# Prompt attention: probabilities turned against a diagonal of reciprocals, values as weights

## The chip, the cores and the metric

One core of one Trainium2 chip runs the whole program. The metric is the device time of one execution in microseconds (us), the median of several. The core's engines are TensorE (PE in the rows, its weight loads PEld), VectorE (DVE), ScalarE (ACT), GpSimd (POOL) and SyncE (SP), which issues most DMAs; each runs its own instruction list in order and waits on semaphores.

## The reference

Two hybrid decoder layers for a prompt of 528 rows (16 learned + 512) and 64 sample rows. In each layer the prompt's attention is two head groups over the same queries:

```
# sparse group (DSA), 8 heads x 64, one shared K/V head
score = sum over 8 index heads of w * relu(q_idx . k_idx), causal; keep the top_k = 528 // 4 = 132 best
s = q . k * 64**-0.5, keys not chosen -> -inf
o_a = softmax(s) @ v                      # v: 64 wide
# latent group (MLA), 8 heads, latent 128
s = (q_lat . c_kv + q_pe . k_pe) * scale, causal
o_lat = softmax(s) @ c_kv                 # 128 wide
o_b = o_lat @ w_uv                        # 128 -> 64 per head
mix = concat(o_a, o_b) @ w_o
```

## The kernel before, in words

A layer runs as blocks with a barrier of all engines between them: the index block, `prompt_block`, two sample blocks, the dense block. The change is in `prompt_block` alone, which is passed twice (once a layer). Between two blocks GpSimd clears a range of semaphores.

`prompt_block` cuts the 528 query rows into tiles t = 0..3 of 128 rows and t = 4 of 16 rows; tile t sees (t+1) x 128 keys. A *group* is a kind and a tile ("M" latent, "D" sparse), in the order M0, D0, M1, D1, ... M4, D4. A *unit* is one head of one group, so 8 units a group (one for t = 4, where the 8 heads lie stacked in the rows): 66 units a layer. A table `plan` sets the order by hand. In iteration i every engine does its part of several units:

- PE: sometimes an index product for a later tile (L1720), the scores of unit i (L1739 to L1745), the *turn* of unit i-1 (L1754: the exponentials `pP` transposed with the identity, one matmul per 128 keys), the *sum* of unit i-2 (L1772: weights are the turned probabilities `pPT`, values move through; out comes rows x values). At a group's end it also turns the group's scaled outputs (`posb`, L1791) and, for M, multiplies with `wuv` (L1783).
- DVE: row maximum of unit i (L1916); *rounds* that find the best keys of a later D group (L1883, L1885, eight a round, 0 to 2 rounds a unit by a table); at a group's end reciprocals of the 8 row sums (L1928) and the scaling of all 8 heads' outputs (L1937, L1933); a step of the sample group's selection in 14 units (L1478, L1481); the low parts `xtl` (L1865).
- ACT: relu of the index product (L1826), exponential with row sum of unit i (L1833), copy of the turned unit i-1 (L1843), copies `polT` (L1854) and `xth` (L1808) at group ends.
- POOL: weights and adds the index scores in 24 units of t = 0 and 1 (L1665, L1668, L1671), then, once PE has reached the last M3 unit, issues the gather of the first cache page for the next block (L1674, recorded as L1980).

Score products use two PSUM slots in turn, turned blocks two others, and the sums lie in banks 6 and 7. The exponentials have three buffers, `pPT` two.

The lines that order the turn and the sum:

```
1751  e.wait_ge(S.s_read, plan[u]["s"] + 1)      # turn of u waits for its exponential
1754  mm = e.transpose(BB(q)[0:kr, ...], Pb[:, u % 3, k * P:k * P + kr], T.ident[:, :])
1761  e.wait_ge(S.o_done, o_free[kind, t])       # first sum of a group waits for the scaling
```

Of the kernel before, what the change touches and what calls it, by code (L numbers as in the profile page):

```python
# [5 lines left out]
F32 = mybir.dt.float32  # L6
# [8 lines left out]
P = 128  # L15
# [924 lines left out]
def proj_stage(nc, T, S, l, W, O, B, S0_, ln_e):  # L940
# [50 lines left out]
    if True:  # L991
# [307 lines left out]
        def tensor(e):  # L1299
# [142 lines left out]
            for name, b, who in TURNS[JOB["ql2"]:]:  # L1442
# [45 lines left out]
def prompt_block(nc, T, S, next_cache):  # L1488
# [36 lines left out]
    osb = T.M.put("posb", [P, 1024], F32, A.region(4096))  # L1525
# [10 lines left out]
    rinv = T.M.put("prinv", [P, 2, 9], F32, A.region(72))  # L1536
# [24 lines left out]
    lag = n + 6  # L1561
    for i in range(lag):
        p = dict(idx=None, dots4=None, sum4=None, s=None, t=[], pv=None, norm=None, ot=[], uv=None)
# [19 lines left out]
        if i - 2 in last:  # L1583
            p["norm"] = last[i - 2]
        if i - 4 in last and last[i - 4][0] == "M":
            p["uv"] = (b_job, last[i - 4][1])
            b_kind.append("X")
            b_job += 1
        if i - 3 in last:
            kind, t = last[i - 3]  # L1590
            for a in range(2 if kind == "M" and t < 4 else 1):
                p["ot"].append((b_job, kind, t, a))
                b_kind.append("O" if kind == "M" else "X")
                b_job += 1
        plan.append(p)
    tjob = {i - 1: p["t"][-1] for i, p in enumerate(plan) if p["t"]}
    ot_job = {(kind, t): q for p in plan for q, kind, t, a in p["ot"]}
# [30 lines left out]
    with nc.Block() as block:  # L1628
# [10 lines left out]
        def _(e):  # L1639
# [11 lines left out]
            for i, p in enumerate(plan):  # L1651
# [3 lines left out]
                if p["idx"]:  # L1655
# [10 lines left out]
                    else:  # L1666
# [4 lines left out]
                        e.tensor_tensor(sc, sc, re, ALU.add).then_inc(S.scored, 1)  # L1671

# [4 lines left out]
        def _(e):  # L1677
# [15 lines left out]
            for i, p in enumerate(plan):  # L1693
# [53 lines left out]
                for part, q in enumerate(p["t"]):  # L1747
                    u = i - 1
                    kind, t, h = units[u]
                    if part == 0:  # L1750
                        e.wait_ge(S.s_read, plan[u]["s"] + 1)
                    b_free(e, q)
                    for k, kr in key_tiles(t)[4:] if part else key_tiles(t)[:4]:
                        mm = e.transpose(BB(q)[0:kr, (k % 4) * P:(k % 4 + 1) * P], Pb[:, u % 3, k * P:k * P + kr], T.ident[:, :])  # L1754
                    mm.then_inc(S.b_ps, 1)
                if p["pv"] is not None:
# [10 lines left out]
                    for k, kr in kts:  # L1767
                        if k < 4:
                            v = T.z[0:kr, k, at_v:at_v + w]
                        else:  # L1770
                            v = vt[0:16, 0:AD] if kind == "D" else vt[0:16, AD:AD + RL]
                        mm = e.matmul(flat[:, o:o + w], PT[0:kr, u % 2, k * P:(k + 1) * P], v,  # L1772
                                      start=k == kts[0][0], stop=k == kts[-1][0])
                    mm.then_inc(S.pv_done, 1)
                if p["uv"]:
# [3 lines left out]
                    e.wait_ge(S.b_out, sum(1 for x in b_kind[:ot_job["M", t] + 1] if x != "X"))  # L1779
# [6 lines left out]
                for q, kind, t, a in p["ot"]:  # L1786
                    e.wait_ge(S.o_done, at[kind, t] + 1)
                    b_free(e, q)
                    for k in range(4 if t < 4 else 1):
                        c = (4 * a + k) * P  # L1790
                        mm = e.transpose(BB(q)[:, k * P:(k + 1) * P], osb[:, c:c + P], T.ident[:, :])  # L1791
                    mm.then_inc(S.b_ps, 1)

        def mix(q, kind, t):

            cols = slice(QC[t], QC[t] + QT[t])
            if (kind, t) == ("D", 4):
                return [((half_rows(u), slice(0, 4), cols), BB(q)[half_rows(u), 64 * u:64 * u + 64].rearrange("p (k c) -> p k c", k=4))
                        for u in range(2)]
            return [((slice(0, P), slice(4, 8) if kind == "M" else slice(0, 4), cols),  # L1800
                     BB(q).rearrange("p (k c) -> p k c", k=4)[:, :, 0:QT[t]])]

        @block.scalar
        def _(e):
            def mix_hi(q, kind, t):
                e.wait_ge(S.b_ps, q + 1)
                for to, src in mix(q, kind, t):
                    ins = e.activation(T.xth[to], src, ACT.Copy)  # L1808
                ins.then_inc(S.mix_hi, 1)

            for i, p in enumerate(plan):
# [23 lines left out]
                for part, q in enumerate(p["t"]):  # L1835
# [8 lines left out]
                    else:  # L1844
                        e.activation(PT[0:16, u % 2, 512:PW], BB(q)[0:16, 0:P], ACT.Copy).then_inc(S.b_out, 1)
                if p["uv"]:
                    mix_hi(p["uv"][0], "M", p["uv"][1])
                for q, kind, t, a in p["ot"]:
                    if kind == "D":
                        mix_hi(q, kind, t)  # L1850
                    else:
                        e.wait_ge(S.b_ps, q + 1)
                        nh = 4 if t < 4 else 1
                        e.activation(olT[:, 4 * a:4 * a + nh, :], BB(q)[:, 0:nh * P].rearrange("p (k c) -> p k c", k=nh), ACT.Copy)\  # L1854
                         .then_inc(S.b_out, 1)
# [1013 lines left out]
```

## Time and profile before

| | us |
|---|---|
| median of 3 runs (lowest, highest) | 3161.12 (3158.76, 3161.49) |
| the profiled execution | 3156.46 |
| its span | 3154.7 |
| first prompt block in it | 644.4 to 832.2, 187.8 |
| second prompt block begins, next block's first work | about 2195, 2385.2 |

Over the whole span PE is busy 93%, DVE 45%, ACT 32%, POOL 20%; the granted clock of PE is 9 tenths or more nearly everywhere. The prompt blocks are a different program from the rest: there PE and DVE work in turns on short instructions, so a share over the span tells little about them. They are read from windows and timelines of the first block; the second repeats it row by row (the row maximum at 819.70 of the first stands at 2372.70 in the second).

### The profile page before, as it was taken

What the parts mean: (1) busy time and instruction counts of PE and PEld (TensorE: products, weight loads), DVE (VectorE), ACT (ScalarE), POOL (GpSimd) and SP (SyncE); (2) the same over time, 40 slices, a digit from 0 to 9 for tenths busy, and PEclk for the clock granted to TensorE, in tenths of its full rate; (3) what the DMA queues carried; (4) which work ended last, traced back from release to release, by engine and by line L of the source; (5) the groups of instructions that cost most, each with busy time, mean ns of one, the idle gap of its engine ahead of it and who ended that gap; (6) DMA issues with size and microseconds to landing.
All of it is one profiled execution on the core that took longest, in us unless ns stands there. A gap on an engine that the chain in (4) does not pass through costs nothing. (4 is left out here: it accounts for less than half of the span.)

```text
span 3154.7 us, 45592 instructions
## 1 busy us (share of the span) xinstructions
PE 2939.6 (93%) x18282; PEld 2524.9 (80%) x18298; DVE 1413.7 (45%) x2118; ACT 998.4 (32%) x1620; POOL 643.3 (20%) x562
## 2 busy tenths in 40 slices
PE   7999999888898899999999999998888988999997
PEld 7999879755566689998799997795656666999975
DVE  2222255579764442223632223735887445222236
ACT  2222233454443332222422222334444333122223
POOL 1111021330113141110221110412302123211103
PEclk9999999999999999999999999999999999999998
DMA  4222452400123322224422224423002234222243
GB/s 118 80 80 80 134 158 79 144 1 1 68 86 131 107 87 80 80 80 135 160 87 80 80 86 141 144 62 134 1 18 80 74 113 147 73 80 79 88 147 124
DMA packets 241737, 293.79 MB, mean 93 GB/s; under 512 B 12624, under 2 KB 205488, under 8 KB 235456
## 3 DMA queue, kind: packets, MB, share of 16 engines
q1 hardware_dynamic: 234688, 229.00, 23.6%
q0 software_dynamic: 6912, 62.92, 5.4%
q8 instruction: 91, 1.49, 0.2%
q14 instruction: 46, 0.38, 0.0%
HBM read 287.72 MB, written 3.88 MB: 92 GB/s over the span
## 5 line engine op out<-in xcount | busy, mean ns | idle before, releaser
L159 DVE TENSOR_TENSOR wlo<-raw,whi 128x1024 fp32r<-128x1024 f32 (+2 forms) x398 | 515.0, 1295 | 1298.1 <-ACT whi L153 1296.9
L153 ACT ACTIVATE whi<-raw 128x1024 fp32r<-128x1024 f32 (+2 forms) x398 | 418.6, 1053 | 1438.7 <-PE ps L608 864.8
L608 PE MATMUL ps<-xth,whi 128*128 128x296 f32 x2624 | 752.2, 299 | 5.4 <-PEq L770 5.4
L608 PE MATMUL ps<-xtl,whi 128*128 128x296 f32 x2624 | 754.7, 300 | 0.0
L608 PE MATMUL ps<-xth,wlo 128*128 128x296 f32 x2624 | 571.7, 300 | 0.0
L608 PEld LDWEIGHTS ps<-xth,whi 128*128 128x128 f32 x2624 | 494.7, 189 | 5.5 <-issue 5.5
L608 PEld LDWEIGHTS ps<-xtl,whi 128*128 128x128 f32 x2624 | 493.5, 188 | 0.0
L608 PEld LDWEIGHTS ps<-xth,wlo 128*128 128x128 f32 x2624 | 427.5, 188 | 0.0
L166 PE MATMUL ps<-whi,hth 128*128 128x512 f32 (+1 forms) x880 | 350.6, 398 | 10.0 <-DVE wlo L159 8.4
L168 PE MATMUL ps<-whi,htl 128*128 128x512 f32 (+1 forms) x880 | 346.9, 394 | 0.0
L167 PE MATMUL ps<-wlo,hth 128*128 128x512 f32 (+1 forms) x880 | 346.7, 394 | 0.0
L575 POOL CAST hth<-hf 128x592 f32 x88 | 59.8, 680 | 930.3 <-DVE hf L534 889.6
L166 PEld LDWEIGHTS ps<-whi,hth 128*128 128x128 f32 (+1 forms) x880 | 158.5, 180 | 67.8 <-DVE wlo L159 22.2
L168 PEld LDWEIGHTS ps<-whi,htl 128*128 128x128 f32 (+1 forms) x880 | 158.2, 180 | 45.9
L167 PEld LDWEIGHTS ps<-wlo,hth 128*128 128x128 f32 (+1 forms) x880 | 158.4, 180 | 42.1
L166 PE MATMUL ps<-whi,xth 128*128 128x338 f32 (+3 forms) x370 | 135.7, 367 | 15.1 <-DVE wlo L159 13.1
L262 POOL TENSOR_SCALAR x<-x,rstd,nb 128x1024 f32<-128x1024 f32 (+2 forms) x24 | 30.7, 1278 | 560.6 <-DVE nb L253 560.6
L577 POOL TENSOR_TENSOR htl<-hf,hth 128x592 f32 x88 | 129.4, 1470 | 14.5 <-POOL hth L575 14.5
L167 PE MATMUL ps<-wlo,xth 128*128 128x338 f32 (+3 forms) x370 | 130.9, 354 | 0.0
L168 PE MATMUL ps<-whi,xtl 128*128 128x338 f32 (+3 forms) x370 | 130.8, 354 | 0.0
L1833 ACT ACTIVATE pP<-ps,pnmx 128x128 f32<-128x128 f32 (+3 forms) x132 | 70.3, 533 | 182.1 <-DVE pnmx L1916 182.1
L1772 PE MATMUL ps<-z,pPT 128*128 128x128 f32 (+1 forms) x672 | 97.6, 277 | 10.8 <-DVE posb L1937 10.8
(407 smaller groups left out, 4348.0 us busy)
## 6 DMA issues: line engine op xcount, KB each, us to landing
raw<-in_ffn_w_in SPq DMA_DIRECT2D x176, 512.0 KB, 3.8
raw<-in_ffn_w_out SPq DMA_DIRECT2D x176, 512.0 KB, 3.5
raw<-in_w_o SPq DMA_DIRECT2D x32, 512.0 KB, 3.4
raw<-in_w_in SPq DMA_DIRECT2D x16, 507.0 KB, 3.9
gb<-in_ln_g SPq DMA_DIRECT2D x6, 512.0 KB, 5.6
gb<-in_ln_b SPq DMA_DIRECT2D x6, 512.0 KB, 6.4
raw<-in_w_in SPq DMA_DIRECT2D x8, 338.0 KB, 3.1
x<-in_x_prompt SPq DMA_DIRECT2D x1, 1536.0 KB, 10.7
```

Of the source, the lines that this page charges most:

```text
L153: e.activation(dst, T.raw[:, s, 0:width], ACT.Copy).then_inc(S.hi_done, 1)
L159: e.tensor_tensor(w_lo, T.raw[:, s, 0:width], w_hi.bitcast(F32), ALU.subtract).then_inc(S.split_done, 1)
L166: e.matmul(out, lhi, rhi, start=start, stop=False)
L167: e.matmul(out, lhi, rlo, start=False, stop=False)
L168: return e.matmul(out, llo, rhi, start=False, stop=stop)
L262: e.tensor_scalar(x, x, T.rstd[0:r, t:t + 1], T.nb[0:r, t:t + 1], ALU.mult, ALU.add).then_inc(S.norm_done, 1)
L575: e.tensor_copy(h_hi, T.hf[:, u, :]).then_inc(S.hhi_done, 1)
L577: e.tensor_tensor(h_lo, T.hf[:, u, :], h_hi.bitcast(F32), ALU.subtract).then_inc(S.hlo_done, 1)
L608: mm = e.matmul(bank(u, up)[:, h, :], part[:, s, w], xp[:, k, o], start=(k == 0 and part is T.whi and xp is T.xth), stop=(k == KD - 1 and ...
L1772: mm = e.matmul(flat[:, o:o + w], PT[0:kr, u % 2, k * P:(k + 1) * P], v, start=k == kts[0][0], stop=k == kts[-1][0])
L1833: e.activation(Pb[:, i % 3, 0:NK[t]], SB(p["s"], P, NK[t]), ACT.Exp, bias=nmx[:, i % 3:i % 3 + 1], accum_out=rsum[:, a, c:c + 1]).then_inc ...
```

## The change

Per unit: DVE takes the reciprocal of the unit's row sum right behind the unit's exponential; POOL multiplies the identity with it into a 128x128 diagonal `pdiag` (three buffers); PE's turn becomes a full float32 product of `pP` (weights) with that diagonal, so the probabilities come out turned and already scaled. The sum then takes the values as weights and the turned probabilities as the moving side, so outputs come out turned. At group ends the scaling on DVE, `posb` and its turns on PE are gone; ACT copies from the sums' banks straight to `polT` (M) or `xth` (D). The product with `wuv` comes one iteration earlier. The prompt block's semaphores are now aliased on the dense block's set, not the sample block's.

```diff
@@ PE
                     if part == 0:
-                        e.wait_ge(S.s_read, plan[u]["s"] + 1)
+                        e.wait_ge(S.diag_done, u + 1)
                     b_free(e, q)
                     for k, kr in key_tiles(t)[4:] if part else key_tiles(t)[:4]:
-                        mm = e.transpose(BB(q)[0:kr, (k % 4) * P:(k % 4 + 1) * P], Pb[:, u % 3, k * P:k * P + kr], T.ident[:, :])
+                        mm = e.matmul(BB(q)[0:kr, (k % 4) * P:(k % 4 + 1) * P], Pb[:, u % 3, k * P:k * P + kr], diag[:, u % 3, :],
+                                      start=True, stop=True)
...
-                    if h == 0 and o_free[kind, t] > 0:
-                        e.wait_ge(S.o_done, o_free[kind, t])
+                    if h == 0:
+                        sums_free(e, kind, t)
...
-                        mm = e.matmul(flat[:, o:o + w], PT[0:kr, u % 2, k * P:(k + 1) * P], v,
-                                      start=k == kts[0][0], stop=k == kts[-1][0])
+                        for out, c in sums(kind, t, h):
+                            mm = e.matmul(out, v, PT[0:kr, u % 2, k * P + c.start:k * P + c.stop],
+                                          start=k == kts[0][0], stop=k == kts[-1][0])
...
-                for q, kind, t, a in p["ot"]:
-                    e.wait_ge(S.o_done, at[kind, t] + 1)
-                    b_free(e, q)
-                    for k in range(4 if t < 4 else 1):
-                        c = (4 * a + k) * P
-                        mm = e.transpose(BB(q)[:, k * P:(k + 1) * P], osb[:, c:c + P], T.ident[:, :])
@@ new: where a sum goes (D: even heads to rows 0-63, odd to 64-127), and what its bank waits for
+    def sums(kind, t, h):
+        if t == 4:
+            if kind == "M":
+                return [(flat[:, 7 * 512:7 * 512 + P], slice(0, P))]
+            return [(flat[half_rows(u), 6 * 512:6 * 512 + 64], half_rows(u)) for u in range(2)]
+        if kind == "M":
+            return [(flat[:, 6 * 512 + h * P:6 * 512 + (h + 1) * P], slice(0, P))]
+        c = 6 * 512 + h // 2 * P
+        return [(flat[half_rows(h % 2), c:c + P], slice(0, P))]
+    def sums_free(e, kind, t):
+        if (kind, t) == ("M", 4):
+            e.wait_ge(S.ol_out, 8)
+        elif kind == "D" and t < 4:
+            e.wait_ge(S.ol_out, 2 * t + 1)
+        elif t > 0:
+            e.wait_ge(S.d_lo, t)
+            if kind == "M":
+                e.wait_ge(S.ol_out, 2 * t)
@@ POOL, at the end of every iteration and ahead of the page gather
+                if i < n:
+                    e.wait_ge(S.rinv_done, i + 1)
+                    e.tensor_scalar(diag[:, i % 3, :], T.ident[:, :], rinv[:, i % 3:i % 3 + 1], 1.0, ALU.mult, ALU.mult)\
+                     .then_inc(S.diag_done, 1)
@@ ACT: sums_out at a group's end
+                e.wait_ge(S.pv_done, i - 1)
+                if kind == "D":
+                    e.activation(T.xth[to], src, ACT.Copy).then_inc(S.d_hi, 1)
...
+                    for a in range(2):
+                        e.activation(olT[:, 4 * a:4 * a + 4, :], T.ps[:, 6 + a, :].rearrange(...), ACT.Copy).then_inc(S.ol_out, 1)
@@ DVE
+                    of, k = rounds.get(units[i], (0, 0))
+                    now = min(k, 1)
                     if units[i] in rounds:
-                        now = 1 if p["norm"] else k
                         choose(of, now, i == starts[of], i == ends[of] and now == k)
-                if p["norm"]:
...
+                    e.wait_ge(S.s_read, p["s"] + 1)
+                    if i >= 3:
+                        e.wait_ge(S.diag_done, i - 2)
+                    e.reciprocal(rinv[:, i % 3:i % 3 + 1], rsum[:, a, c:c + 1]).then_inc(S.rinv_done, 1)
+                if p["out"] and p["out"][0] == "D":
+                    mix_lo(None, *p["out"], S.d_hi, S.d_lo)
                 if i < n:
-                    if p["norm"] and units[i] in rounds and now < k:
+                    if now < k:
                         choose(of, k - now, False, i == ends[of])
@@ build
-        prompt_s, index_s, init_s = (Again(sample_s, names) for names in (PROMPT_SEMS, INDEX_SEMS, INIT_SEMS))
+        index_s, init_s = (Again(sample_s, names) for names in (INDEX_SEMS, INIT_SEMS))
+        prompt_s = Again(dense_s, PROMPT_SEMS)
```

PE's order from the last M3 unit into D3, before (`pP` exponentials, `pPT` turned ones, `posb` scaled outputs, `z` values):

```order
L1744 MATMUL ps<-kT_89,qaT 128x512
L1745 MATMUL ps<-pbias,identb 128x512
L1754 MATMUL ps<-ident,pP 128x128 x4
L1772 MATMUL ps<-z,pPT 128x64 x4
L1791 MATMUL ps<-ident,posb 128x128 x8
```

The same place in the changed kernel:

```order
L1757 MATMUL ps<-pkeys_3858,qaT 128x512
L1758 MATMUL ps<-pbias,identb 128x512
L1767 MATMUL ps<-pdiag,pP 128x128 x4
L1786 MATMUL ps<-pPT,z 128x128 x4
L1757 MATMUL ps<-kT_89,qaT 128x512
L1758 MATMUL ps<-pbias,identb 128x512
L1767 MATMUL ps<-pdiag,pP 128x128 x4
L1786 MATMUL ps<-pPT,z 64x128 x4
L1797 MATMUL ps<-polT,wuv 64x128 x8
L1757 MATMUL ps<-pkeys_3858,qaT 128x512
```

The turn reads `pdiag`, the sum has its operands exchanged, the eight turns of `posb` are gone and the product with `wuv` stands one iteration earlier.

DVE in units M3 h0 and h1, before:

```order
L1916 TENSOR_REDUCE pnmx<-ps 128x1
L1878 TENSOR_TENSOR pwork_3845<-pwork_3845,trib 16x16
L1883 MAX ptop<-pwork_3845 16x8
L1885 MATCH_REPLACE pwork_3845<-ptop,pwork_3845 16x532
L1883 MAX ptop<-pwork_3845 16x8
L1885 MATCH_REPLACE pwork_3845<-ptop,pwork_3845 16x532
L1916 TENSOR_REDUCE pnmx<-ps 128x1
L1883 MAX ptop<-pwork_3845 16x8
L1885 MATCH_REPLACE pwork_3845<-ptop,pwork_3845 16x532
L1928 RECIPROCAL prinv<-prsum 128x8
L1937 TENSOR_TENSOR posb<-ps,prinv 128x512
```

And changed:

```order
L1924 TENSOR_REDUCE pnmx<-ps 128x1
L1886 TENSOR_TENSOR pwork_3845<-pwork_3845,trib 16x16
L1891 MAX ptop<-pwork_3845 16x8
L1893 MATCH_REPLACE pwork_3845<-ptop,pwork_3845 16x532
L1934 RECIPROCAL prinv<-prsum 128x1
L1891 MAX ptop<-pwork_3845 16x8
L1893 MATCH_REPLACE pwork_3845<-ptop,pwork_3845 16x532
L1924 TENSOR_REDUCE pnmx<-ps 128x1
L1891 MAX ptop<-pwork_3845 16x8
L1893 MATCH_REPLACE pwork_3845<-ptop,pwork_3845 16x532
L1934 RECIPROCAL prinv<-prsum 128x1
L1874 TENSOR_TENSOR xtl<-ps,xth 128x4x128
```

Every unit has a reciprocal behind its first round; the scaling is gone, and D2's low part follows in h1.

POOL at the end of the block, before:

```order
L1671 TENSOR_TENSOR pwork<-pwork,prelu 128x512
L1654 MEMSET pwork_3845 128x4
L1980 DMA pg<-in_cache_mla,rows 128x2560
L1628 UNCONDITIONAL_BRANCH
L1951 ISA
```

And changed:

```order
L1683 TENSOR_SCALAR pdiag<-ident,prinv 128x128 x13
L1663 MEMSET pwork_3845 128x4
L1683 TENSOR_SCALAR pdiag<-ident,prinv 128x128 x22
L1974 DMA pg<-in_cache_mla,rows 128x2560
L1637 UNCONDITIONAL_BRANCH
```

The gather of the next block's page stands behind the last diagonal.

## Rows read from the trace of the kernel before

**Rows 1.** Windows: us, PE, PEld, DVE, ACT, POOL busy (count), PEclk, DMA, GB/s.

```profile
644.40:678.17 33.77, 28.15 (x166) 20.78 (x167) 23.10 (x58) 17.56 (x65) 17.01 (x32) 0.90 0.01 1
678.17:717.90 39.73, 36.04 (x209) 25.41 (x208) 34.24 (x92) 21.27 (x63) 20.26 (x23) 1.00 0.01 1
717.90:745.26 27.36, 21.21 (x115) 13.95 (x114) 26.15 (x60) 8.81 (x26) 0.10 (x1) 1.00 0.00 1
745.26:766.53 21.27, 19.76 (x132) 14.01 (x133) 18.08 (x38) 11.36 (x29) 0.00 (x0) 1.00 0.01 2
766.53:794.56 28.03, 26.34 (x139) 16.65 (x139) 27.14 (x52) 10.52 (x26) 1.05 (x1) 1.00 0.10 33
794.56:820.45 25.89, 22.32 (x147) 15.53 (x148) 21.94 (x39) 11.82 (x28) 0.00 (x0) 1.00 0.04 17
820.45:832.20 11.75, 8.83 (x76) 6.78 (x75) 3.78 (x11) 4.97 (x14) 0.00 (x0) 0.97 0.01 1
644.40:832.20 187.80, 162.65 (x976) 113.09 (x979) 154.43 (x345) 86.31 (x247) 38.42 (x56) 0.98 0.02 8
```

**Rows 2.** Timeline inside group D2: start us, us, engine, line, instruction.

```profile
761.23 0.56 DVE L1916 TENSOR_REDUCE pnmx<-ps 128x1 f32<-128x384 f32 x1
...
761.66 0.86 PE L1744 MATMUL ps<-pkeys,qaT 128*128 128x384 f32 x2
...
761.82 0.58 ACT L1833 ACTIVATE pP<-ps,pnmx 128x384 f32<-128x384 f32 x1 [0.94 <-DVE pnmx L1916]
...
762.30 0.19 ACT L1833 ACTIVATION_READ_ACCUMULATOR pP<-ps,pnmx 128x1 f32 x1
...
762.51 0.68 DVE L1885 MATCH_REPLACE8 pwork<-ptop,pwork 128x516 f32<-128x516 f32 x1
...
762.55 0.55 PE L1754 MATMUL ps<-ident,pP 128*128 128x128 f32 x3
...
762.93 0.88 PE L1772 MATMUL ps<-z,pPT 128*128 128x64 f32 x6
763.22 0.56 DVE L1916 TENSOR_REDUCE pnmx<-ps 128x1 f32<-128x384 f32 x1
```

**Rows 3.** Timeline inside group M3, TensorE.

```profile
784.65 1.02 PE L1739 MATMUL ps<-ckvT,qlatT 128*128 128x512 f32 x2
...
786.42 0.60 PE L1754 MATMUL ps<-ident,pP 128*128 128x128 f32 x4
...
786.87 1.06 PE L1772 MATMUL ps<-z,pPT 128*128 128x128 f32 x8
...
787.76 1.02 PE L1739 MATMUL ps<-ckvT,qlatT 128*128 128x512 f32 x2
```

**Rows 4.** Waits in the block: who waited for whom, us in total, times, longest.

```profile
PE ps L1772 <- DVE posb L1937: 5.4, 6, 1.2
```

**Rows 5.** Groups by line in the block, VectorE: busy us, mean ns, idle before.

```profile
L1937 DVE TENSOR_TENSOR posb<-ps,prinv 128x1024 f32<-128x1024 f32 (+2 forms) x9 | 8.0, 884 | 0.8 <-PE ps L1791 0.5
...
L1928 DVE RECIPROCAL prinv<-prsum 128x8 f32<-128x8 f32 (+1 forms) x10 | 1.9, 195 | 2.9 <-PE ps L1772 2.6
```

**Rows 6.** Groups by line and shape in the block, GpSimd's scoring.

```profile
L1671 POOL TENSOR_TENSOR pwork<-pwork,prelu 128x512 f32<-128x512 f32 x7 | 8.9, 1272 | 0.6
...
L1668 POOL TENSOR_SCALAR prelu<-prelu,iw 128x512 f32<-128x512 f32 x7 | 4.9, 695 | 7.0 <-ACT prelu L1826 7.0
L1668 POOL TENSOR_SCALAR prelu<-prelu,iw 128x384 f32<-128x384 f32 x7 | 4.1, 588 | 4.5 <-ACT prelu L1826 4.5
```

**Rows 7.** GpSimd timeline: the page gather; then the landing of all gathers.

```profile
789.98 1.05 POOL L1980 DMA_INDIRECT pg<-in_cache_mla,rows  x1 [62.37 <-PE ps L1742]
...
DMA to landing us min/median/max: 6.2/6.6/10.3
```

**Rows 8.** The range clear at the end of the prompt block and of the dense block.

```profile
L1951 POOLq EVENT_SEMAPHORE_RANGE_CLEAR  x2: 196/196/196, 831.9 to 2384.9; - x2
...
L2814 POOLq EVENT_SEMAPHORE_RANGE_CLEAR  x3: 588/590/594, 595.8 to 3145.6; - x3
```

More of the change, by code:

```diff
@@ L1524, in prompt_block @@
     relu = T.M.put("prelu", [P, 2, PROMPT], F32, A.region(2 * PROMPT * 4))
-    osb = T.M.put("posb", [P, 1024], F32, A.region(4096))
+    rinv = T.M.put("prinv", [P, 3], F32, A.region(12))
+    diag = T.M.put("pdiag", [P, 3, P], F32, A.region(3 * P * 4))
     olT = T.M.put("polT", [P, 8, P], F32, A.region(4096))
@@ L1583, in prompt_block @@
         if i - 2 in last:
-            p["norm"] = last[i - 2]
-        if i - 4 in last and last[i - 4][0] == "M":
-            p["uv"] = (b_job, last[i - 4][1])
+            p["out"] = last[i - 2]
+        if i - 3 in last and last[i - 3][0] == "M":
+            p["uv"] = (b_job, last[i - 3][1])
             b_kind.append("X")
             b_job += 1
[L1589 to L1594, printed above, removed]
         plan.append(p)
     tjob = {i - 1: p["t"][-1] for i, p in enumerate(plan) if p["t"]}
-    ot_job = {(kind, t): q for p in plan for q, kind, t, a in p["ot"]}
     def b_free(e, q):
@@ L1778, in _ @@
                     b_free(e, q)
-                    e.wait_ge(S.b_out, sum(1 for x in b_kind[:ot_job["M", t] + 1] if x != "X"))
+                    e.wait_ge(S.ol_out, 2 * t + 2 if t < 4 else 9)
                     for h in range(8):
@@ L1845, in _, with mix_lo @@
                         e.activation(PT[0:16, u % 2, 512:PW], BB(q)[0:16, 0:P], ACT.Copy).then_inc(S.b_out, 1)
+                if p["out"]:
+                    sums_out(i, *p["out"])
                 if p["uv"]:
[L1847 to L1855, printed above, removed]
+                    latent_hi(*p["uv"])
         @block.vector
         def _(e):
-            nround, nlo, nsround = [0], [0], [0]
-            def mix_lo(q, kind, t):
-                nlo[0] += 1
-                e.wait_ge(S.mix_hi, nlo[0])
-                for to, src in mix(q, kind, t):
-                    ins = e.tensor_tensor(T.xtl[to], src, T.xth[to].bitcast(F32), ALU.subtract)
-                ins.then_inc(S.mix_lo, 1)
+            nround, nsround = [0], [0]
+            def mix_lo(q, kind, t, high, low):
+                e.wait_ge(high, t + 1)
+                to, src = mix(q, kind, t)
+                e.tensor_tensor(T.xtl[to], src, T.xth[to].bitcast(F32), ALU.subtract).then_inc(low, 1)
             def choose(t, k, start, end):
```

63 lines of the change are left out of this document (20 added, 43 removed).

## The prediction

> **What bounds the kernel now.** The windows by group come first, since both prompt blocks are separate from the rest by barriers: what they gain or lose goes into the time one to one, twice. The reader sees 187.8 us for the first block, PE busy 162.7 and DVE 154.4, ACT 86, POOL 38 [rows 1]. Neither of the two is full, so the wait that ends last changes by group: in M2 DVE is busy 26.15 of 27.36 us and PE 21.2; in D2 both are near (18.1 and 19.8 of 21.3); in M3 27.1 and 26.3 of 28.0.
>
> Second, a timeline inside D2, which shows the beat of one unit. The row maximum starts at 761.23, the next one at 763.22: 1.99 us. In it DVE does maximum and one round back to back, until 763.19, so DVE sets the beat. PE meanwhile does scores from 761.66, turn at 762.55, sum at 762.93. The turn starts 0.06 after the exponential's row sum ended (762.49), and could come no earlier [rows 2]. In M3 PE goes without a pause: scores 784.65, turn 786.42, sum 786.87, next scores 787.76, 3.11 us a unit [rows 3]. There four turns take 0.45, and eight passes of the sum 0.89: 0.111 us a pass of 128 columns.
>
> Third, the waits: `posb` held PE's sums 6 times, 5.4 us in all [rows 4]. That is the stall which the change removes, with the DVE work behind it.
>
> **What is removed, per block.** DVE: the scalings, 8.0 us, and 10 reciprocals, 1.9 us [rows 5]. PE: 50 turns of `posb` at 0.111, 5.5 us, and the 5.4 us of waits. What is late next there: for D groups, an ACT copy and `xtl` in place of reciprocal and scaling, both of which were there before; for M, the ACT copy alone. I give these ends the full DVE gain and no more.
>
> **What is added, per block.**
> 1. *Turns as products.* A turn was one pass per 128 keys (4 in the M3 unit), the float32 sum of the same size is two (8) [rows 3]. The product with the diagonal has the sum's shape, so it takes two: 0.111 more per key block, 160 blocks in t = 0 to 3 and 8 or so in t = 4, 18.6 us of PE. Net of `posb`'s turns PE gets 13 us more work. Sums keep their passes (for D, weights of 128 columns and 64 moving become weights of 64 and 128 moving; six passes of a D2 sum are recorded with 0.88 us [rows 2], eight of an M3 sum with 128 moving with 1.06 [rows 3], so the narrow side saved nothing and its exchange costs nothing).
> 2. *Reciprocals.* 66 on DVE. One costs 0.16 to 0.2 (10 took 1.9, [rows 5]); with its gap I take 0.2: 13.2 us. Net of what is removed: +3.3 us. In a unit without a round DVE now also stands until the exponential is done: in D2 the row sum ends 1.26 us after the maximum began, and the maximum itself takes 0.56 [rows 2]: 0.7 us of standing. Seven units carry a selection step and no round (five in t = 0, two in D3), and what is queued behind is the step and then the next maximum, which ACT and, through ACT, PE wait for.
> 3. *Diagonals.* 66 on POOL. No such instruction is in the trace. By the scoring multiply, 0.695 us for 512 keys and 0.588 for 384 [rows 6], 0.107 per 128, a 128-wide one takes 0.37; its ends are 0.17 (a quarter of the 512-wide one) and 0.59 (the 384-wide one, if width did not matter below it). I take 0.37, since both rows lie on that slope. In 24 units POOL is also scoring: 0.695 + 1.272 ahead of the diagonal at 512 keys.
> 4. *The longer way to the turn.* This decides. Before: from a unit's maximum to its turn 1.32 us (761.23 to 762.55, [rows 2]). Now: maximum and round until 763.19 (1.96), reciprocal 0.2, diagonal 0.37, two hand-overs of 0.06: 2.65 us. PE then does turn, sum and the scores of the unit after the next, and only these give DVE its next maximum. So two beats cannot be shorter than 2.65 + turn 0.67 + sum 0.67 + scores 0.89 + 0.1 = 4.98, one beat 2.49, where it was 1.99.
>
> **Group by group**, per block, by the longest of DVE's work, PE's work and the loop of point 4:
> - D2 (21.27): DVE 1.99 + 0.2 = 2.2 a unit, PE 0.89 + 0.33 + 0.67 + 0.33 = 2.2, loop 2.49. Six units at +0.5, less the scaling at M2's end: a scaling and its reciprocal take 0.88 + 0.2 = 1.1 on average [rows 5], after an M group, twice as wide, I take 1.4, after a D group 0.8; about half of it is on the path here, since the loop now ends last: **+2.2**.
> - M3 (28.03): PE 3.11 + 0.44 = 3.55 a unit, 28.4 for eight, and it still stands about 1 us while DVE has its units of two rounds; DVE has 27.1 - 0.8 + 1.6 = 27.9. So 29.3: **+1.3**.
> - D3 (25.89): the loop is 2.8 + 0.89 + 0.89 + 1.1 + 0.1 over two, 2.9, against 2.1 of DVE (D2's 1.99 and 0.1 for the wider maximum) in three units without a step, +2.4; standing 0.7 in two, +1.4; less the scaling 1.4, the 8 turns of `posb` 0.9, and 1.1 of posb's waits: **+0.4**.
> - M2 (27.36): DVE bound; 8 x 0.2 less 0.85: **+0.8**.
> - t = 1 (39.73): 16 reciprocals 3.2, less 2.3 for the scalings; PE +3.5 of passes less 1.3; in D1 POOL needs 1.97 + 0.37 + gaps, 2.5 us a unit, where the mean was 2.6 with units at 2.0. **+2.7**, between -1 and +7.
> - t = 0 (33.77): five step units at 0.7, reciprocals 3.2, passes 1.8, less 1.5; the product of these hides half: **+3.2**, between 0 and +5.
> - t = 4 (11.75): the way M4, D4 to the end loses two scalings and two turns with their hand-overs, and gains longer turns (1.1) and diagonals: **-0.8**.
> - The clear of semaphores between blocks: 0.196 us for the prompt block's set, 0.590 for the dense one, which it now shares [rows 8]: **+0.4**.
> - The page gather moves from 789.98 to behind the last diagonal, some 6 us before the block's end; it lands 6.2 to 10.3 us after its issue, median 6.6 [rows 7]. What waits for it is the next block's first instructions on PE and ACT. At the median it is just late, **+0.1**; at 10.3 +3.8.
>
> Sum 10.3 us a block, 20.6 for two. The ends, taken together, are -4 and +28 a block: t = 0 and 1 as given (-1, +12), the other terms between what DVE alone gives them (-3 in all) and every unit at its loop with a diagonal of 0.59 and the late page (+16). The profiled execution took 3156.5, so 3177.1; the median of the runs stands 4.6 above it, and I forecast for that: **3181 us**, +0.65%.
>
> The trace's price of a turn, one pass against two, is what I use, and its block gives 18.6 us of added PE work. The Trainium skill (page "TensorE: Matmul & The Clock Gate", Terms) says of the transpose mode that it is 4x faster for FP32; by that rule the lost mode would cost three more passes each, 56 us a block, which is a rival below. Another page, "TensorEngine Tiling (Array Packing)", When to Use Tiling, names just this exchange: with a 64-wide right side, swap the operands and get two column tiles. By it D's sums, 80 key blocks of two passes, would cost half, 8.9 us of PE less a block. No row shows it here, and heads whose halves differ stand a whole iteration apart in PE's order, so I count nothing for it.
>
> **The rivals.**
> - *A. PE's passes hide and the group ends pay: faster.* PE is idle 25 of 187.8 us, DVE 33 [rows 1]. If the diagonal is always there when PE comes to the turn (it stands behind the next unit's scores, 0.9 to 1.8 us), the loop never closes, the +13 of PE and +3 of DVE fit into the idle time, and 5.4 of waits, and about 3 of the DVE chains at group ends, go: -8 a block, 3145. It decides from a way to the turn under 1.6 us in D2 (two beats of 1.99 less 2.33). Against it: the round alone takes 1.96. 7%.
> - *B. Only work counts, not the way.* PE-bound units pay (M3, D1, D3, half of D2), the loop is slack since some units carry two rounds or a step: +3 to +5 a block, 3167 to 3171. For it: the mean beats of M2, D3 and M3 are 3.2 to 3.5 [rows 1], longer than any loop. 20%, a third of it within 0.2%.
> - *C. POOL's queue and the late page.* The diagonal at 0.59, behind scoring of 1.97, closes every loop in t = 0 and 1, and the page lands late: +18 a block, 3197. For it: POOL was never on the path and is now in each unit. 12%.
> - *D. The turn at four times.* 56 us of PE a block on 162.7 - 5.5 gives 213 where 187.8 stood: +25 a block, 3211 or more. Against it: eight passes against four in [rows 3]. 3%.
> - *The forecast*, +12 to +30 in all: 55%. What is left, 3%, is no change because terms cancel.
>
> A difference within 0.2%, 6 us, can't be told from none. Faster 7%; within it 10% (7 of B, 3 of the rest); slower 83%. Range 3165 to 3199: it leaves out A, the low third of B and the upper part of C with D.
>
> **What the changed profile would show.** Turns of 8 passes in t = 3 with 0.9 us between turn and sum; reciprocals of 0.16 us, diagonals of about 0.37 on POOL; the turn waiting for POOL (`pdiag`) in D2 and D1, and not in M2; D2's beat near 2.5 and M3's near 3.55; the block near 198 us; the first PE or ACT instruction of the sample block waiting for `pg`. I am wrong if D2's beat stays at 2.0, if turns have four passes, or if a block is shorter than 187.8.

## The result, and the profile after

| | before | changed |
|---|---|---|
| median, us (lowest to highest, runs) | 3160.97 (3158.76 to 3161.49, 4) | 3184.91 (3184.13 to 3187.47, 4) |
| ratio, 95% interval | | 1.008 (1.0069 to 1.0092) |
| profiled execution, its span | 3156.46, 3154.7 | 3184.53, 3182.8 |

The change costs 24 us: slower by 0.8%, inside the range of 3165 to 3199 and 4 above the 3181 forecast. The spans of the two profiled executions differ by more, 28.1 us, because the profiled one of the kernel before was 4.5 us faster than its median. The two prompt blocks hold 26.6 of the 28.1, 14.9 and 11.7. In the experiments below, two of z2's eleven executions took 4867 and 4869 us at a granted clock of 0.56 and stay out of its ratio; all others lie within 0.5% of the fastest of their kernel.

The windows of the first prompt block, cut at the same places as in [rows 1] (columns as there):

```profile
643.54:680.44 36.90, 30.99 (x173) 21.87 (x173) 23.32 (x72) 17.83 (x64) 22.94 (x48) 0.91 0.01 1
680.44:722.75 42.31, 40.40 (x226) 28.27 (x224) 34.13 (x104) 21.61 (x63) 25.83 (x39) 1.00 0.01 1
722.75:750.24 27.49, 23.38 (x139) 16.95 (x138) 25.97 (x66) 8.91 (x26) 2.97 (x8) 1.00 0.00 1
750.24:775.44 25.20, 23.56 (x146) 15.71 (x146) 17.86 (x44) 11.46 (x29) 3.02 (x9) 1.00 0.01 2
775.44:805.06 29.62, 28.80 (x164) 19.94 (x166) 27.33 (x58) 10.50 (x26) 2.97 (x8) 1.00 0.00 1
805.06:832.55 27.49, 27.19 (x175) 19.19 (x176) 21.71 (x45) 11.81 (x28) 2.97 (x8) 1.00 0.00 1
832.55:846.20 13.65, 9.62 (x95) 7.11 (x93) 2.17 (x6) 4.75 (x13) 1.79 (x3) 0.99 0.28 97
643.54:846.20 202.66, 183.93 (x1106) 129.04 (x1109) 152.49 (x390) 86.86 (x246) 62.48 (x122) 0.98 0.02 8
```

PE took 21 us more work, the removed turns of `posb` already taken off, where I had 13 (the surplus is taken up below). DVE's busy time fell by 2 although it runs 66 reciprocals. The block grew by 15 us, among its single groups most in D2 (+3.9), least in M2 (+0.1).

D2's timeline, the stretch that answers to [rows 2] (start, us, engine, line, instruction, in brackets the idle time before it and who ended it):

```profile
765.34 0.56 DVE L1924 TENSOR_REDUCE pnmx<-ps 128x1 f32<-128x384 f32 x1 [0.32 <-PE ps L1758]
...
767.33 0.16 DVE L1934 RECIPROCAL prinv<-prsum 128x1 f32<-128x1 f32 x1
767.59 0.37 POOL L1683 TENSOR_SCALAR pdiag<-ident,prinv 128x128 f32<-128x128 f32 x1 [2.10 <-DVE prinv L1934]
...
768.12 0.83 PE L1767 MATMUL ps<-pdiag,pP 128*128 128x128 f32 x6
768.32 0.56 DVE L1924 TENSOR_REDUCE pnmx<-ps 128x1 f32<-128x384 f32 x1 [0.82 <-PE ps L1758]
...
768.88 0.87 PE L1786 MATMUL ps<-pPT,z 128*64 128x128 f32 x6
...
769.68 0.91 PE L1757 MATMUL ps<-pkeys,qaT 128*128 128x384 f32 x2
...
770.79 0.56 DVE L1924 TENSOR_REDUCE pnmx<-ps 128x1 f32<-128x384 f32 x1 [0.32 <-PE ps L1758]
```

This is the loop of the prediction's point 4, closed: maximum 765.34, turn 768.12 (2.78 later, forecast 2.65), sum 0.76 later, scores 0.80 after that, the next maximum but one 1.11 after those, at 770.79. Two units take 5.45, one 2.72, where the row maxima of [rows 2] stood 1.99 apart.

M3, answering to [rows 3], has eight passes in the turn, 1.0 us from turn to sum and 3.72 us from scores to scores where it was 3.11. Seven of the eight passes take 0.11 us from start to start; the first, whose weight load waited for the diagonal, takes 0.21:

```profile
788.07 1.02 PE L1752 MATMUL ps<-ckvT,qlatT 128*128 128x512 f32 x2
...
789.90 1.16 PE L1767 MATMUL ps<-pdiag,pP 128*128 128x128 f32 x8
790.90 1.06 PE L1786 MATMUL ps<-pPT,z 128*128 128x128 f32 x8
791.79 1.02 PE L1752 MATMUL ps<-ckvT,qlatT 128*128 128x512 f32 x2
```

The waits of the block (who waited for whom, us, times, longest). The `posb` wait of [rows 4] is gone, the turn waits for GpSimd's diagonal instead:

```profile
PEld ps L1767 <- POOL pdiag L1683: 26.9, 39, 2.1
PE ps L1767 <- POOL pdiag L1683: 12.6, 21, 1.7
DVE prinv L1934 <- ACT pP L1849: 8.7, 15, 0.9
```

The groups of DVE and POOL that stand in place of [rows 5] (busy us, mean ns):

```profile
L1934 DVE RECIPROCAL prinv<-prsum 128x1 f32<-128x1 f32 x66 | 10.8, 164 | 10.5 <-ACT pP L1849 8.7 <-DVE pwork L1893 0.2
```

```profile
L1683 POOL TENSOR_SCALAR pdiag<-ident,prinv 128x128 f32<-128x128 f32 x66 | 24.7, 374 | 125.6 <-DVE prinv L1934 125.4
```

The diagonal costs the 0.37 forecast, the reciprocal the lower end of its 0.16 to 0.2. At the block's end GpSimd issues the gather at 837.76, DVE's last work ends at 842.69, and nothing runs until 846.2. The rows of the barrier (duration min/median/max in ns, first and last start) and the sample block's first instructions:

```profile
L1945 POOLq DRAIN  x2: 46/46/46, 845.2 to 2410.7; - x2
...
L1945 POOLq EVENT_SEMAPHORE_RANGE_CLEAR  x2: 590/590/590, 845.5 to 2410.9; - x2
```

```profile
837.76 1.04 POOL L1974 DMA_INDIRECT pg<-in_cache_mla,rows  x1 [0.15 <-issue]
...
846.24 0.29 PEld L2341 LDWEIGHTS ps<-ident,pg 128*128 128x128 f32 x2 [4.17 <-issue]
846.25 1.06 ACT L2523 ACTIVATE Mks<-pg 128x1024 fp32r<-128x1024 f32 x1 [3.81 <-PEq L1945]
846.27 1.24 DVE L1478 MAX8 slist<-swork 128x8 f32<-128x1032 f32 x1 [3.58 <-PEq L1945]
```

All engines start together behind the barrier, DVE too, which doesn't read the page. GpSimd's drain at the barrier stands at 845.2, 7.4 us after the gather's issue. Just before it lies another, at the block's end, and the trace shows what that one waits for. It runs from 837.2 for 7.85 us (second block: 2403.4, 7.06 us); the gather lands 7.19 us after its issue at 837.76 (second block 6.41 after 2403.99). So the drain ends 0.09 and 0.08 us behind the landing (the second line below is of the first block's gather alone, from issue to landing):

```profile
L1637 POOLq DRAIN  x2: 7062/7456/7850, 837.2 to 2403.4; - x2
...
DMA to landing us min/median/max: 7.2/7.2/7.2
```

### The profile page after: what moved, and what is told of

Same layout as the page of the kernel before. It is cut to its first block and busy times, and to the rows that moved or that the text cites. A ratio compares the mean times of both kernels' runs of the same rounds, so it can differ in the third digit from the quotient of the medians.

```text
span 3182.8 us, 46374 instructions
## 1 busy us (share of the span) xinstructions
PE 2984.2 (94%) x18542; PEld 2559.7 (80%) x18558; DVE 1409.2 (44%) x2208; ACT 999.0 (31%) x1618; POOL 689.4 (22%) x694
## 5 line engine op out<-in xcount | busy, mean ns | idle before, releaser
L166 PEld LDWEIGHTS ps<-whi,hth 128*128 128x128 f32 (+1 forms) x880 | 158.6, 180 | 67.6 <-DVE wlo L159 22.1
L262 POOL TENSOR_SCALAR x<-x,rstd,nb 128x1024 f32<-128x1024 f32 (+2 forms) x24 | 30.6, 1276 | 560.6 <-DVE nb L253 560.6
L1767 PEld LDWEIGHTS ps<-pdiag,pP 128*128 128x128 f32 x680 | 87.5, 192 | 63.3 <-POOL pdiag L1683 53.7
L1767 PE MATMUL ps<-pdiag,pP 128*128 128x128 f32 x680 | 108.2, 291 | 25.7 <-POOL pdiag L1683 25.0
L577 POOL TENSOR_TENSOR htl<-hf,hth 128x592 f32 x88 | 129.0, 1466 | 14.5 <-POOL hth L575 14.5
## 6 DMA issues: line engine op xcount, KB each, us to landing
x<-in_x_prompt SPq DMA_DIRECT2D x1, 1536.0 KB, 10.6
```

Of the source, the lines that this page charges most:

```text
L166: e.matmul(out, lhi, rhi, start=start, stop=False)
L262: e.tensor_scalar(x, x, T.rstd[0:r, t:t + 1], T.nb[0:r, t:t + 1], ALU.mult, ALU.add).then_inc(S.norm_done, 1)
L577: e.tensor_tensor(h_lo, T.hf[:, u, :], h_hi.bitcast(F32), ALU.subtract).then_inc(S.hlo_done, 1)
L1767: mm = e.matmul(BB(q)[0:kr, (k % 4) * P:(k % 4 + 1) * P], Pb[:, u % 3, k * P:k * P + kr], diag[:, u % 3, :], start=True, stop=True)
```

## The experiments

The theory: the change has four parts with separate prices, (1) group ends without scaling, `posb` and its wait, a gain; (2) the reciprocals; (3) the turn's second pass; (4) the turn's wait over DVE and POOL; and (5), a cost at the block's end from the gather. Rivals: only work costs and the wait is slack (B), GpSimd's queue (C).

All lengths below are read from the first prompt block's trace, between the starts of the groups' first row maxima; "end" runs from M4's to the next block's first work. The second block's lie within 0.5 us of them, except the kernel before's t = 0 and D3 (32.6 and 27.2) and the ends with a late gather (x5 14.4, x3 13.8, x2 13.9, changed 13.7). "exp" is the exponential.

| us | before | x6 | x5 | x3 | x2 | changed | z1 |
|---|---|---|---|---|---|---|---|
| passes a turn; turn waits for | 1; exp | 1; exp | 1; exp | 2; exp | 1; diagonal | 2; diagonal | 1; scaled exp, a unit later |
| t=0 | 31.5 | 30.6 | 33.0 | 33.3 | 34.6 | 34.7 | 33.1 |
| t=1 | 39.6 | 39.0 | 39.3 | 40.7 | 40.9 | 42.2 | 38.5 |
| M2 | 27.4 | 27.0 | 27.4 | 27.4 | 27.4 | 27.5 | 27.4 |
| D2 | 21.2 | 20.4 | 20.4 | 22.7 | 23.2 | 25.1 | 20.3 |
| M3 | 28.0 | 27.7 | 28.0 | 28.6 | 28.6 | 29.6 | 28.0 |
| D3 | 25.9 | 23.4 | 23.6 | 26.7 | 25.1 | 27.5 | 23.8 |
| end | 12.6 | 10.6 | 13.1 | 14.8 | 13.2 | 14.5 | 11.7 |
| sum | 186.1 | 178.6 | 184.8 | 194.2 | 192.9 | 201.0 | 182.8 |
| median of runs | 3161 | 3140.4 | 3156.2 | 3171.7 | 3172.6 | 3184.9 | 3151.3 |

**x1, the gather early.** Of the changed kernel, only the place of the gather is another: inside the loop, behind the diagonal of the last M3 unit.

```diff
+                if i == first_unit["M", 3] + 7:
+                    e.wait_ge(S.s_ps, p["s"] + 1)
+                    page_load(e, T, 0, T.pg[:, 0, :, :], next_cache, 0)
```

> The changed kernel, but the gather of the next block's first page is issued right behind the diagonal of unit M3 h7, as before the change, and not behind the last diagonal. End theory (the barrier waits for this gather to land, 2 us a block): the first instruction of the sample block 0.8 to 1.3 us behind the last one of the prompt block (3.5 in the changed kernel), 1.3 to 2.3 us a block saved, total 3180 to 3182. Rival (the barrier is longer only by the wider clear, 0.4 us): total 3184 to 3185, gap unchanged.

Measured 3178.52, ratio to before 1.0054 (1.004 to 1.0068), 6.4 us under the changed kernel. From the last work to the next block's first it has 1.26 and 1.27 us, where the changed kernel has 3.58 and 2.79; before had 0.87. The 0.39 that stays is the larger clear of [rows 8]; the gather's place costs 2.3 and 1.5 us here. GpSimd's drain at the block's end, 7.85 and 7.06 us in the changed kernel, is short again, since the gather landed long before:

```profile
L1637 POOLq DRAIN  x2: 584/585/586, 837.9 to 2402.0; - x2
```

The end theory holds, but the total fell 1.5 us below its range: only 3.8 of the 6.4 us stand at the block's ends, the rest I cannot place.

**x2, one pass, with the wait; x3, two passes, without it.**

```diff
 x2
-  e.matmul(BB(q)..., Pb[...], diag[:, u % 3, :], start=True, stop=True)
+  e.transpose(BB(q)..., Pb[...], T.ident[:, :])
 x3
-  e.wait_ge(S.diag_done, u + 1)
+  e.wait_ge(S.s_read, plan[u]["s"] + 1)
-  e.matmul(BB(q)..., Pb[...], diag[:, u % 3, :], start=True, stop=True)
+  e.matmul(BB(q)..., Pb[...], T.ident[:, :], start=True, stop=True)
```

> The changed kernel, with the turn against the identity in transpose mode again (one pass), still behind the diagonal's semaphore; the diagonal is made and not used, so the probabilities are left unscaled. Loop theory (the way over DVE and POOL sets the beat, passes only in M3 and D3): turns shorter by 0.33 to 0.44 shorten each loop by that over two units; D2's beat 2.3, M3 DVE-bound at 3.4; 4 to 6 us a block saved, total 3173 to 3177. Passes theory (PE's added work alone costs): all 12 us a block gone, total near 3161.

> The changed kernel, with the turn a product with the identity (two passes, as in the change) that waits for the exponential alone; reciprocals and diagonals are still made beside it, but nothing waits for them, and the probabilities are left unscaled. Loop theory: D2's beat back to 2.2, set by PE's work, M3 stays at 3.55; 4 to 6 us a block saved, total 3173 to 3177. Passes theory: nothing saved, total 3183 to 3185.

Measured 3172.63, ratio 1.0038 (1.0025 to 1.0052), and 3171.72, ratio 1.0037 (1.0022 to 1.0051). Both kernels came a little below the 3173 to 3177 of the loop theory, and far from the passes theory's totals. Against x5, which has neither, the wait costs 16.4 us and the pass 15.5; both together 28.7. So they nearly add: 3 us less than the sum, which is less than single executions of x2 differ by (3169.7 to 3175.2). In the traces of the two blocks adding up is short by 1.4 and 0.1 us. They sit in different places: the wait most in D2 (2.9 in the first block), the pass in D3 (3.1) and D2 (2.3). In D2 of x3 PE never stops:

```profile
762.84 0.83 PE L1767 MATMUL ps<-ident,pP 128*128 128x128 f32 x6
763.60 0.87 PE L1786 MATMUL ps<-pPT,z 128*64 128x128 f32 x6
764.40 0.91 PE L1757 MATMUL ps<-pkeys,qaT 128*128 128x384 f32 x2
765.15 0.33 PE L1758 MATMUL ps<-pbias,identb 128*128 128x384 bf16 x1
765.31 0.83 PE L1767 MATMUL ps<-ident,pP 128*128 128x128 f32 x6
```

A unit is 2.47 of pure PE work (I had 2.2). In x2 PE stands, the turn opened by the diagonal, and two units take 5.06:

```profile
760.68 0.56 DVE L1923 TENSOR_REDUCE pnmx<-ps 128x1 f32<-128x384 f32 x1 [0.74 <-PE ps L1758]
...
763.35 0.55 PE L1767 MATMUL ps<-ident,pP 128*128 128x128 f32 x3 [0.55 <-POOL pdiag L1683]
...
765.74 0.56 DVE L1923 TENSOR_REDUCE pnmx<-ps 128x1 f32<-128x384 f32 x1 [0.74 <-PE ps L1758]
```

**x4, the kernel before with two passes**, the turn as a product with the identity, nothing else.

```diff
-  e.transpose(BB(q)..., Pb[...], T.ident[:, :])
+  e.matmul(BB(q)..., Pb[...], T.ident[:, :], start=True, stop=True)
```

> The kernel before, with only its turn of the probabilities as a float32 product with the identity (two passes for one). Passes theory: +10 to +12 us a block, total 3181 to 3185. Loop theory: passes are paid where PE is near its bound (D1, D2, M3, D3): D2 at 2.2 a unit, M3 at 3.55; +3 to +5 us a block, total 3167 to 3171.

Measured 3174.18, ratio 1.0046 (1.0029 to 1.0062): about 13 us for the second pass alone, here too, with an interval of 9 to 20. It lies between the two ranges, 3 us above the loop theory's and 7 below the passes theory's, so neither had its size. In the first block the four groups that the loop theory names (D1, D2, M3, D3) pay 4.8 us, nearly half of it in D3, and t = 4, which it doesn't name, 1.5.

**x5, x2 and x3 together: one pass, no wait** (reciprocals and diagonals are made, nobody on the path waits for them). **x6, x5 without them,** and with the gather early.

```diff
 x6, beside x5's edits
-  e.reciprocal(rinv[:, i % 3:i % 3 + 1], rsum[:, a, c:c + 1]).then_inc(S.rinv_done, 1)
-  e.tensor_scalar(diag[:, i % 3, :], T.ident[:, :], rinv[...], 1.0, ALU.mult, ALU.mult)
```

> The changed kernel with both of the last two edits: the turn in one pass against the identity, and behind the exponential alone. Reciprocals and diagonals are made beside it, nothing waits for them; the probabilities are left unscaled. If passes and way add up (12 and 13 us of the whole each): total 3159 to 3163. If they are two bounds of the same units, so that either alone leaves the other: more than their sum goes, total below 3158. If the second buys nothing once the first is gone: 3170 to 3173.

> As x5, and the reciprocals and diagonals are left out altogether: what is left of the change is its group ends (no scaling on DVE, no turns of the outputs, sums with exchanged operands) and the wider clear; the gather is issued early again, since nothing holds GpSimd. The probabilities are left unscaled. Forecast's terms (66 reciprocals at 0.2 us where DVE is the bound, the wait for the gather 3 us a block): 6 to 12 us below x5, total 3149 to 3156, so that the group ends alone would have gained 2 to 6 us a block. Rival (posb's waits were hidden anyway): total 3158 to 3162.

Measured 3156.19, ratio 0.9989 (0.9981 to 0.9998), and 3140.37, ratio 0.994 (0.9927 to 0.9954). x5 lies 3 us below its range for adding up, on the side of two bounds of the same units; by the comparison above that overlap is small, if there is any. x6 lies 9 us below its range. What the change removes is thus worth 20.7 us, net of the wider clear, where I had expected at most 12; the two blocks show 7.5 and 9.9 of it, the rest lies outside them. Of the 15.8 us between x5 and x6, about 6 are the gather (2.5 and 3.8 at the block's ends). The rest, 9 to 10, goes to reciprocals and diagonals, which x6 leaves out together, so that they are not separated. Most of it is in t = 0 (2.3 in the first block), where DVE stands 5.8 us for the exponential in x5. In D2 they cost nothing, x5 and x6 both have 20.39: there PE sets the beat in both, 2.13 us.

**x7, GpSimd scales the exponentials in place,** one-pass turn, gather early.

```diff
-  e.tensor_scalar(diag[:, i % 3, :], T.ident[:, :], rinv[...], 1.0, ALU.mult, ALU.mult)
+  e.tensor_scalar(kr_, kr_, rinv[...], 1.0, ALU.mult, ALU.mult)   # kr_: Pb[:, i % 3, 0:NK[t]]
```

> All of the result computed: GpSimd multiplies the exponentials themselves with the reciprocals, in place (128 x 128(t+1), 0.37 to 0.70 us instead of 0.37), and the turn is a transpose in one pass again; the gather is issued early. Loop theory: the way grows by 0.1 to 0.33 a unit, the turn shrinks by as much, and PE loses the 18.6 us a block: total 3166 to 3171, 8 to 12 us under x1 (3178.5), still above the kernel before. Rival (GpSimd's queue closes the loop in t = 0 and 1, where it also scores): total 3175 or more.

Measured 3170.19, ratio 1.003 (1.0018 to 1.0041). The pass is saved, but GpSimd takes 0.58 us at 384 keys in place of 0.37, on the path: D2 is 24.0.

**y1, D's sums with 128 columns of weights** instead of 64, in the changed kernel.

```diff
-  v = T.z[0:kr, k, at_v:at_v + w]
+  v = T.z[0:kr, k, at_v:at_v + (P if t < 4 else w)]
-  return [(flat[half_rows(h % 2), c:c + P], slice(0, P))]
+  return [(flat[:, c:c + P], slice(0, P))]
```

> The changed kernel, but D's sums use 128 columns of weights (the values and what stands beside them) and write all 128 partitions of the bank, so that no matmul of t = 0 to 3 but wuv's is in half the array; what is added up in the odd heads' rows is overwritten and not the result. Same number of passes. Theory (each change between half and full width costs PE an overlapped weight load, 0.1 us, two a D unit: turn and sum of D2 take 0.80 for six passes, in M3 0.89 for eight): D1, D2 and D3 each 1 to 2 us shorter, total 3175 to 3180. Rival (0.133 a pass comes from elsewhere): no change, 3184 to 3186.

Measured 3181.24, ratio 1.0065 (1.0052 to 1.0079). The intervals overlap, so the times alone don't settle it; the trace does. A unit of D2 in which PE doesn't stop:

```profile
766.10 0.81 PE L1757 MATMUL ps<-kT,qaT 128*128 128x384 f32 x2
766.74 0.33 PE L1758 MATMUL ps<-pbias,identb 128*128 128x384 bf16 x1
766.90 0.83 PE L1767 MATMUL ps<-pdiag,pP 128*128 128x128 f32 x6
767.57 0.83 PE L1786 MATMUL ps<-pPT,z 128*128 128x128 f32 x6
768.24 0.81 PE L1757 MATMUL ps<-pkeys,qaT 128*128 128x384 f32 x2
```

Read beside D2 of x3 above, where D's sums have 64 columns of weights and PE doesn't stop either: turn to sum 0.67 for 0.76, sum to scores 0.67 for 0.80, scores to turn 0.81 for 0.91, the unit 2.15 for 2.47. So the passes of the turn are no slower in D than in M. What costs is each change between 128 and 64 columns of weights: 0.09 us before the sum, 0.13 in it and up to the scores, 0.10 in these, 0.32 a D unit. D2 drops to 24.3, D3 to 26.5, t = 1 to 41.5. That is less than the 1 to 2 us a group that I expected, and the total lies above the expected range too. In D2 every second unit still stands for its diagonal: the beats are 2.15 and 2.98 in turn, where they were 2.47 and 2.98.

**z1, x7 with the turn a unit later; z2, x1 with the turn a unit later.** The same edit in both:

```diff
-        if 0 <= i - 1 < n:                     # turn
+        if 0 <= i - 2 < n:
-        if 0 <= i - 2 < n:                     # sum; group end and wuv product likewise
-            p["pv"] = i - 2
+        if 0 <= i - 3 < n:
+            p["pv"] = i - 3
```

> As x7_pool_scales (GpSimd multiplies the exponentials in place by the reciprocal, one-pass transpose, sums and group ends as in the changed kernel, gather early), and the turn of a unit stands one iteration later in PE's order, the sum, the copies and the wuv product with it. It computes the full result. My theory (the way over VectorE and GpSimd to the turn is what costs, not their work): with a whole unit in between the way is hidden, so the time is that of x5_one_pass_no_wait (3156.2) less the early page (about 6), plus 1 to 2 us a block for one more iteration of emptying at the end: 3150 to 3156, D2 at 20.4 to 20.8 us and D3 at 23.6 to 24.2 where x7 had 24.0 and 25.9. Rival (GpSimd's own work in each unit, 0.38 to 0.69 us, slows its neighbours or becomes the beat): no better than x7, 3167 to 3172, D2 near 24.

> As x1_page_early (the changed kernel, its product with the diagonal included, gather early), and the turn of a unit stands one iteration later in PE's order, the sum, the copies and the wuv product with it. It computes the full result. My theory: the wait goes (about 8 us a block in x2 against x5), the second pass stays (about 7.8 us a block in x3 against x5): x3_no_wait (3171.7) less the page (6) plus 2 to 3 for emptying: 3165 to 3170, still slower than the kernel before; D2 22.5 to 23, M3 28.6. Rival (passes and wait overlap, so that taking away one leaves the other's cost): 3174 to 3180.

z1: 3151.3, ratio 0.9969 (0.9957 to 0.9981), D2 20.3, D3 23.8. z2: 3167.63, ratio 1.0024 (1.0014 to 1.0033), D2 22.1, M3 28.5. Both came where the theory of the way had them: the wait is gone and the work stays. z1 is faster than both kernels, and leaves nothing out. Its D2 (GpSimd's multiply ends before the turn, the maxima 2.13 apart):

```profile
757.42 0.56 DVE L1924 TENSOR_REDUCE pnmx<-ps 128x1 f32<-128x384 f32 x1
757.54 0.58 POOL L1684 TENSOR_SCALAR pP<-pP,prinv 128x384 f32<-128x384 f32 x1 [3.34 <-DVE prinv L1934]
...
759.35 0.49 PE L1768 MATMUL ps<-ident,pP 128*128 128x128 f32 x3
759.55 0.56 DVE L1924 TENSOR_REDUCE pnmx<-ps 128x1 f32<-128x384 f32 x1
```

**z3, the control: the kernel before with the turn a unit later.** The same edit in the kernel before, scaling and `posb` turns with it.

> The kernel before, with only the turn, the sum, the copies, the scaling and the group ends one iteration later. It computes the full result. A control for z1_pool_scales_later, which gained 9 us over the kernel before: does the gain come from the later turn alone? My theory (in the kernel before the turn starts as soon as the exponential is done and VectorE sets the beat, so nothing is gained by standing later, and the group ends stay as they are): within 5 us of before, with 1 to 2 us a block lost at the end, 3158 to 3166, D2 between 20.8 and 21.3. Rival (the loop over the turn binds in the kernel before too): D2 under 20.6, and 3150 to 3155.

Measured 3168.76, ratio 1.003 (1.0021 to 1.004). The plain beat stays 1.98, as expected, so the later turn alone is no gain; but it is no matter of a few us of emptying either: the total lies 3 us above the upper end that I expected, 8.5 above the kernel before. D2 has 24.1 where 21 was expected, and one unit in it takes 6.13 (3.92 before). There PE stands for `posb` twice as long as before (9.5 us of such waits in the block against 5.4), and then it runs at half the clock (windows; PEclk is the third number from the right):

```profile
753.00:755.80 2.80, 1.83 (x14) 1.50 (x14) 2.39 (x5) 1.58 (x4) 0.00 (x0) 1.00 0.00 0
755.80:759.10 3.30, 3.30 (x7) 1.09 (x7) 0.00 (x0) 1.20 (x2) 0.00 (x0) 0.50 0.02 5
```

3.3 us at 1.2 GHz instead of 2.4 are 1.6 us lost, by estimate, about half of what D2 has too much. In D3 808 to 812 is at 0.50 and 812 to 816 at 0.77, and it takes 28.3 us; in the second block it has no such stretch and takes 25.5.

## Why the prediction was right, and where it was not

The direction and the mechanism held: a gain at the group ends, and above it the pass and the way over two engines. That the number came within 4 us is in part luck. The first block grew by 14.9 us against 10.3 forecast, the second by 11.7, because there the kernel before itself lost 1.0 us in t = 0 and 1.3 in D3 to stretches at half the clock (D3 below). Execution against execution, 3184.5 came where 3177.1 was forecast; the 4.6 us that I added for the median are in the kernel before alone. Point by point, first block, forecast against the traces:

- *t = 0* +3.2: +3.1. *t = 1* +2.7: +2.6. *M3* +1.3: +1.6.
- *D2* +2.2: **+3.9**. The loop was right in form and each link was short: the way 2.78 for 2.65, of which 0.11 is the turn's first weight load, which waits for the diagonal too; turn 0.76 and sum 0.80 for 0.67 each, scores to the maximum 1.11 for 0.99. Every pass inside the turn takes the 0.11 that I had; the surplus stands where the columns of weights change.
- In the same point, *the exchange of the D sums costs nothing* was wrong. I read it from recorded durations (0.88 against 1.06), which contain the matmul's modelled end; measured from start to start, y1 gives 0.09 before the sum, 0.13 for it and 0.10 behind it. x6, with no reciprocal at all, shows D2's plain beat at 2.13, not 1.99: with these 0.32 PE, and no longer DVE, sets it.
- *PE's work* +13: **+21** busy. Most of the surplus is the narrow sums: y1, which has them at full width, is busy 178.4, 5.6 less. x6 says the same, with 162.7 as before although the 50 turns of `posb` are gone. The rest I have not split.
- *M2* +0.8: **+0.1**. The eight reciprocals went into DVE's own idle time. I had also said that the turn wouldn't wait there; it waits more than in any other group (6.9 us of PEld's), and it costs nothing: x2 with the wait and x5 without it both have 27.4, and DVE is busy 26.0 of 27.5 in the changed kernel.
- *D3* +0.4: **+1.6**, in the second block +0.3. The second is not another mechanism: in it the kernel before itself is 1.3 us longer, with the clock at 0.94 in place of 1.00:

```profile
794.56:820.45 25.89, 22.32 (x147) 15.53 (x148) 21.94 (x39) 11.82 (x28) 0.00 (x0) 1.00 0.04 17
2347.51:2374.70 27.19, 24.13 (x151) 16.49 (x151) 20.69 (x37) 11.80 (x27) 0.00 (x0) 0.94 0.00 1
```

- *t = 4, clear and gather*, -0.3 in all: **+1.9**. t = 4 itself was right (-0.8 until the last work), and so was the clear (0.39); all of the miss is the gather, +2.3 for +0.1. The gather was sized as a wait of the page's readers, against the median landing of 6.6 us after issue, and just late. The barrier itself stands until 7.4 (second block 6.7) after the issue, for every engine, and then come clear and start. The price, 1.5 to 2.3 a block, lies within the 0.1 to 3.8 that I had for a late page, but I had counted the 0.1.

These errors add up to 4.6 us in the first block, nearly all one way: D2, D3 and the gather too cheap, only M2 too dear.

Rival A had the loop open; x5 shows that even then the block is only 1 to 2 us shorter than before, not 8: the ends' gain of 20 us is real, and reciprocals, diagonals and gather eat 16 of it. Rival B is refuted by x2: with the work of x5 and the wait added, 16.4 us more. Rival C had the diagonal at 0.59 (0.374 measured) and the loops of t = 0 and 1 closed by GpSimd's scoring; t = 1 grew by 2.6 only. Rival D: x4 and x3 put the lost mode at one pass more per 128 keys, 13 to 15.5 us for the kernel, so twice the passes and not four times. The Trainium skill's 4x for FP32 ("TensorE: Matmul & The Clock Gate", Terms) is not what these turns show. Nor does its swap with two column tiles ("TensorEngine Tiling (Array Packing)", When to Use Tiling) give anything here: the heads of a pair stand a unit apart, nothing runs beside, and y1 shows the half-wide sums dearer.

Open: why a change between 128 and 64 columns of weights costs PE 0.1 us each time; y1 shows that it does, not by what. Open too are 2.6 of x1's 6.4 us, and how the 9 to 10 us between x5 and x6 split between reciprocals and diagonals.

## What to carry to other kernels

Before a product on a tight two-unit loop takes a new operand, add up the way of this operand over all engines and ask whether a whole unit of other work fits between: here the same work cost 19 us more when the turn stood one unit too early (x7 against z1). The shift is no gain by itself: in the kernel before, where the turn didn't wait for a second engine, it cost 8.5 us (z3). A scaling removed at a group's end is paid for in every unit, so count units against groups. And an indirect gather belongs well ahead of a barrier, even where nobody reads it yet.

## What the runs showed of the hardware

- The barrier between blocks came 7.4 and 6.7 us after GpSimd's last gather was issued, with all other work done 2.5 us before (changed kernel, first block). GpSimd's drain at the block's end lasted until 0.08 to 0.09 us after the gather had landed; with the gather issued early it took 0.58 us (x1).
- Six float32 passes of 128 columns with 64 columns of weights, between products with 128, took 0.80 us, with 128 columns of weights throughout 0.67. The six passes ahead of them took 0.76 against 0.67, the product behind them 0.91 against 0.81 (x3, y1). Single passes away from these borders took 0.11 in all of them.
- A float32 transpose of 128 x 128 took one pass of 0.11 us, a float32 product of the same shape two (M3: 0.45 us for four, 1.0 for eight, a late first weight load included).
- After PE had stood for about 1.5 us in D2 of z3, with short waits around it, the granted clock was 0.50 for 3.3 us. There the stop cost once for itself and, by estimate, 1.6 us more for what ran at half speed behind it. In the changed kernel D2 has no such stretch: its three windows from 752 to 761 are at 1.00, although one unit there takes 4.33 us.
